# Head of a hybrid-trunk kernel: squares of the input on two engines, meta tokens turned last, a semaphore of its own for the first weight half

## What is computed

```python
meta = jnp.broadcast_to(meta_tokens[None].astype(x.dtype), (bsz, N_META, D_MODEL))
h = jnp.concatenate([meta, x], axis=1)
...
u = rms_norm(h, mix_norm_g[i])          # h * rsqrt(mean(h*h) + eps) * gain, row by row
z = h @ w_in                            # in conv_pool_mixer, on u
a = a_in[..., :CONV_DIM] * jax.nn.sigmoid(a_in[..., CONV_DIM:])
```

## Time and profile before

| | |
|---|---|
| median of 3 runs | 1159.05 us (1157.74 to 1159.46) |
| the profiled execution, its own time | 1157.56 us |
| its span, first to last instruction | 1155.8 us, mean granted TensorE clock 0.994 |
| TensorE matmul busy | 1128.4 us, 98% of the span |
| first matmul of the first projection | 16.19 us after the span's start |

### The profile page before, as it was taken

How to read it: one execution, slowest core, us unless ns; L and a number is a source line. 1 busy time by engine, 2 the same in 40 slices (tenths; PEclk the granted TensorE clock), 3 DMA queues, 4 the chain that set the end, 5 groups by cost and what they waited for, 6 DMA issues and landing times.

```text
span 1155.8 us, 18677 instructions
## 1 busy us (share of the span) xinstructions
PE 1128.4 (98%) x7817; PEld 1050.6 (91%) x7817; DVE 757.6 (66%) x1063; ACT 526.5 (46%) x826; POOL 2.3 (0%) x30
## 2 busy tenths in 40 slices
PE   6999999999999999999999999999989999999997
PEld 6999999999999999999999888787889899899886
DVE  5898887786785785455353345655786786785443
ACT  6435555454454454333443133543454454454332
POOL 0000000000000000000000000000000000000000
PEclk9999999999999999999899999999999999999999
DMA  6322022233224224222113212132224224224311
GB/s 200 111 74 73 1 74 74 74 107 113 74 93 128 74 81 139 91 93 74 57 54 109 74 43 68 37 109 73 73 74 146 73 74 145 74 86 134 109 37 73
DMA packets 98832, 100.29 MB, mean 87 GB/s; under 512 B 2786, under 2 KB 95644, under 8 KB 98748
## 3 DMA queue, kind: packets, MB, share of 16 engines
q1 hardware_dynamic: 98684, 99.02, 27.2%
q10 hardware_dynamic: 64, 0.07, 0.0%
HBM read 96.99 MB, written 2.10 MB: 86 GB/s over the span
## 4 chain that ended last, share of the span: by engine, by line
PE 81%; DVE 8%; ACT 5%; issue 4%; DMA 1%; SPq 0%; DVEq 0%; ACTq 0%
PE ps L1710 48%; PE ps L1897 20%; PE ps L1963 5%; PE ps L1826 3%; DVE relu L1368 2%; ACT w_hi L487 2%; PE ps L2005 1%; PE ps L2020 1%; DVE w_lo L494 1%; ACT w_hi L525 1%; PE ps L1758 1%; ACT c_hi L877 1%; PE ps L1718 1%; ACT parts L890 1%; DMA raw<-in_cp_w_in_dram 1%
## 5 line engine op out<-in xcount | busy, mean ns | idle before, releaser
L1710 PE MATMUL ps<-u_lo,w_hi 128*128 128x272 f32 (+1 forms) x1120 | 299.6, 323 | 2.2 <-DVE u_lo L1206 2.2
L1710 PE MATMUL ps<-u_hi,w_hi 128*128 128x272 f32 (+1 forms) x1120 | 296.0, 320 | 0.0
L1710 PE MATMUL ps<-u_hi,w_lo 128*128 128x272 f32 (+1 forms) x1120 | 295.6, 320 | 0.0
L494 DVE TENSOR_TENSOR w_lo<-raw,w_hi 128x1024 fp32r<-128x1024 f32 x132 | 161.2, 1224 | 122.5 <-ACT w_hi L487 122.5
L487 ACT ACTIVATE w_hi<-raw 128x1024 fp32r<-128x1024 f32 x132 | 138.4, 1052 | 146.3 <-PE ps L1710 135.4
L1710 PEld LDWEIGHTS ps<-u_lo,w_hi 128*128 128x128 f32 x1120 | 184.4, 189 | 20.2 <-issue 5.2
L1710 PEld LDWEIGHTS ps<-u_hi,w_hi 128*128 128x128 f32 x1120 | 185.2, 190 | 16.1 <-issue 1.2
L1710 PEld LDWEIGHTS ps<-u_hi,w_lo 128*128 128x128 f32 x1120 | 184.1, 188 | 15.4
L1897 PE MATMUL ps<-c_lo,w_hi 128*128 128x264 f32 (+1 forms) x672 | 190.4, 283 | 7.3 <-ACT ps L863 4.8
L1897 PE MATMUL ps<-c_hi,w_lo 128*128 128x264 f32 (+1 forms) x672 | 189.9, 283 | 0.0
L1897 PE MATMUL ps<-c_hi,w_hi 128*128 128x264 f32 (+1 forms) x672 | 189.7, 282 | 0.0
(11 more groups left out here) (239 smaller groups left out, 1550.7 us busy)
## 6 DMA issues: line engine op xcount, KB each, us to landing
raw<-in_ffn_w_dram SPq DMA_DIRECT2D x64, 1024.0 KB, 5.4
raw<-in_gla_w_in_dram SPq DMA_DIRECT2D x12, 1024.0 KB, 5.3
raw<-in_cp_w_in_dram SPq DMA_DIRECT2D x8, 512.0 KB, 5.3
raw<-in_cp_w_out_dram SPq DMA_DIRECT2D x4, 1024.0 KB, 5.0
raw<-in_gla_w_out_dram SPq DMA_DIRECT2D x4, 1024.0 KB, 5.3
xin<-in_x_dram SPq DMA_DIRECT2D x4, 512.0 KB, 5.5
raw<-in_cp_w_in_dram SPq DMA_DIRECT2D x2, 1024.0 KB, 5.0
out_dram<-y_tok SPq DMA_DIRECT2D x4, 512.0 KB, 3.0
```

The source lines that it names most:

```text
L494: dve.tensor_tensor(w_view(w_lo, n), half_view(raw, n), w_view(w_hi, n).bitcast(F32), ALU.subtract).then_inc(w_lo_ready, 1)
L1710: last = mm(ps[:, n % NS, c:c + b - a], l, r[:, a - origin:b - origin], start=(k == 0 and i == 0), stop=(k == count - 1 and i == 2))
```

## The change

VectorE squares the meta tokens and tile 1, ScalarE tiles 0, 2 and 3. VectorE writes its unused squares to `squares_dve`. The scaling of the meta tokens goes to GpSimd, as one tensor_scalar. TensorE transposes tiles 0 to 2 for groups k = 0 to 5 only, then the meta tokens, then tile 3 for k = 0 to 5; the eight transposes of groups 6 and 7 (slot ("x", 3)) stand inside the first projection, in front of its third group. The first half of the first weight block has a semaphore of its own, so `split_hi(0)` waits for this half alone; both `split_hi(0)` and `split_lo(0)` also change places with the meta tokens' pieces.

```diff
@@ raw_count
-    return 16 * (b // 2 + 1 + min(b // 2 + 1, B_POOL // 2))
+    return 16 * (b // 2 + 1 + min(b // 2 + 1, B_POOL // 2) - (b % 2 == 0))
@@ split_hi
-            act.wait_ge(raw_loaded[n // 2 % 2], raw_count(n // 2))
+            if n == 0:
+                act.wait_ge(first_loaded, 16)
+            else:
+                act.wait_ge(raw_loaded[n // 2 % 2], raw_count(n // 2))
@@ load_glu
-                      .then_inc(raw_loaded[c % 2], 16)
+                      .then_inc(raw_loaded[c % 2] if n else first_loaded, 16)
@@ GpSimd, at its end
+            pool.wait_ge(meta_rstd, 1)
+            pool.tensor_scalar(meta_normed, xmeta[:, :], rstd_tok[0:META, TT:TT + 1], None, ALU.mult)\
+                .then_inc(meta_normed_ready, 1)
@@ ScalarE (std_of takes the root of tile j's mean, square squares tile j)
+            square(0)
+            std_of(0, x_squared, 1)
+            n = SLOT["gain",]
+            filled(act, n)
+            act.activation(vec[:, 0:2 * KD], ps[:, n % NS, 0:2 * KD], ACT.Copy).then_inc(evac[n % NS], 1)
+            std_of(1, x_squared_dve, 1)
+            square(2)
+            act.wait_ge(meta_summed, 1)
+            act.activation(std_tok[0:META, TT:TT + 1], ms_tok[0:META, TT:TT + 1], ACT.Sqrt,
+                           bias=eps[0:META, :], scale=1.0 / D).then_inc(meta_std, 1)
+            std_of(2, x_squared, 2)
+            square(3)
+            std_of(3, x_squared, 3)
+            split_hi(0)
+            evacuated(act, SLOT["xm",])
+            act.activation(u_hi[:, :, 0:META], u_meta, ACT.Copy).then_inc(u_meta_hi_ready, 1)
@@ VectorE
+            dve.wait_ge(meta_loaded, 16)
+            V.scalar_tensor_tensor(out=squares_dve[0:META, :], in0=xmeta[:, :], scalar=1.0, in1=xmeta[:, :],
+                                   op0=ALU.mult, op1=ALU.mult, accum_out=ms_tok[0:META, TT:TT + 1])\
+             .then_inc(meta_summed, 1)
+            dve.wait_ge(x_loaded[1], 16)
+            dve.wait_ge(meta_summed, 1)
+            V.scalar_tensor_tensor(out=squares_dve, in0=xin[:, 1, :], scalar=1.0, in1=xin[:, 1, :],
+                                   op0=ALU.mult, op1=ALU.mult, accum_out=ms_tok[:, 1:2])\
+             .then_inc(x_squared_dve, 1)
...
+                if j == 1:
+                    dve.wait_ge(meta_std, 1)
+                    V.reciprocal(rstd_tok[0:META, TT:TT + 1], std_tok[0:META, TT:TT + 1]).then_inc(meta_rstd, 1)
@@ TensorE
+            for j in range(TT):
+                if j == TT - 1:
+                    pe.wait_ge(meta_normed_ready, 1)
+                    n = SLOT["xm",]
+                    for k in range(KD):
+                        last = flip(ps[:, n % NS, META * k:META * (k + 1)], meta_normed[:, P * k:P * (k + 1)], META)
+                    last.then_inc(filled_n, 1)
+                pe.wait_ge(x_normed_ready, j + 1)
+                flip_normed(j, 0, KD - 2)
+
+            def flip_last():
+
+                for j in range(TT):
+                    flip_normed(j, KD - 2, KD)
@@ first projection
-                        input_wait if c == 0 else None)
+                        input_wait if c == 0 else None, flip_last if c == 0 else None, 2)
```

More of the change, by code:

```diff
@@ L326, in build_trunk @@
         x_squared = sem("x_squared")
+        x_squared_dve = sem("x_squared_dve")
         x_std = sem("x_std")
@@ L702, in _, with std_of, square @@
             act.activation(std_head[:, 0:1], eps[:, :], ACT.Sqrt)
[L705 to L711, removed]
+            def std_of(j, squared, count):
+                act.wait_ge(squared, count)
+                act.activation(std_tok[:, j:j + 1], ms_tok[:, j:j + 1], ACT.Sqrt, bias=eps[:, :],
+                               scale=1.0 / D).then_inc(x_std, 1)
+            def square(j):
                 act.wait_ge(x_loaded[j], 16)
@@ L1182, in _ @@
             V.memset(pin[:, :, 0:WMAX], 0.0).then_inc(pin_zeroed, 1)
[L1184 to L1195, removed]
-                                    vec[:, V_MIX:V_MIX + KD, None].to_broadcast([P, KD, META]), ALU.mult)\
-                     .then_inc(evac[n % NS], 1)
+            dve.wait_ge(meta_loaded, 16)
@@ new lines, in _ @@
+            for j in range(TT):
+                dve.wait_ge(x_std, j + 1)
+                V.reciprocal(rstd_tok[:, j:j + 1], std_tok[:, j:j + 1]).then_inc(rstd_tok_ready, 1)
+                dve.wait_ge(rstd_tok_ready, j + 1)
+                V.tensor_scalar(x_normed[:, j, :], xin[:, j, :], rstd_tok[:, j:j + 1], None, ALU.mult)\
+                 .then_inc(x_normed_ready, 1)
+                if j == 1:
+                    dve.wait_ge(meta_std, 1)
+                    V.reciprocal(rstd_tok[0:META, TT:TT + 1], std_tok[0:META, TT:TT + 1]).then_inc(meta_rstd, 1)
@@ L1198, in _ @@
+            n = SLOT["xm",]
+            evacuated(dve, SLOT["gain",])
+            filled(dve, n)
+            V.tensor_tensor(u_meta, ps[:, n % NS, 0:KD * META].rearrange("p (k t) -> p k t", t=META),
+                            vec[:, V_MIX:V_MIX + KD, None].to_broadcast([P, KD, META]), ALU.mult)\
+             .then_inc(evac[n % NS], 1)
+            split_lo(0)
             evacuated(dve, SLOT["xm",])
@@ L1201, in _ @@
              .then_inc(u_meta_lo_ready, 1)
-            split_lo(0)
             for k in range(KD):
@@ L1763, in _, with flip_normed @@
             flip(ps[:, n % NS, 0:2 * KD], gain_rows[:, :], 2 * KD).then_inc(filled_n, 1)
-            pe.wait_ge(x_normed_ready, 1)
-            n = SLOT["xm",]
-            for k in range(KD):
-                last = flip(ps[:, n % NS, META * k:META * (k + 1)], meta_normed[:, P * k:P * (k + 1)], META)
-            last.then_inc(filled_n, 1)
-            for j in range(TT):
-                pe.wait_ge(x_normed_ready, j + 2)
-                for k in range(KD):
+            def flip_normed(j, first, last):
+                for k in range(first, last):
                     n = SLOT["x", k // 2]
```

30 lines of the change are left out of this document (13 added, 17 removed).

## The result

The changed kernel takes 1160.89 us (median of 8 runs, 1159.92 to 1163.58) against 1158.39 us before (8 runs, 1156.06 to 1160.95). The ratio is 1.0024 with a 95% interval of 1.0013 to 1.0035: slower by 2.8 us, or 1.5 to 4.1 (the two medians differ by 2.5). The forecast was 1160.3 us and +1.3. The time lies in its range (1159.4 to 1161.4), but partly by luck: the median of the kernel before came out 0.66 us lower in these 8 runs than in the 3 on which the forecast stood (1159.05). The loss is about double the forecast: it lies just beyond the +0.4 to +2.3 that the forecast had with 0.60, and just beyond the 0.2% whose crossing had 0.20. The profiled execution took 1159.92 us, the lowest of the 8; its span is 1158.1 us, 2.3 more than before.

The account below looks back on a forecast made before the run. TensorE, busy 98% of the span, was taken as the bound, so the first projection's start and TensorE's list count. +0.3 (start) +1.0 (transposes) = +1.3 us: 1160.3 us against the median of the runs, range 1159.4 to 1161.4.

Parts of the forecast that it names:

- What bounds it, and that the shift passes through: TensorE, busy 98% of the span, bounds the kernel; a shift of the first projection moves everything behind it.
- Front of the head: Before the projection: VectorE's squares delay the first large transpose to 8.5 us instead of 8.08, losing 0.4 us.
- GpSimd: Meta scaling in the head: 0.9 to 1.6 us from 9.4, ready by 11.1 and hidden until 12.4.
- The prediction's own sign of being wrong: In the changed profile's head: the forecast is wrong if GpSimd's instruction exceeds 1.85 us.
- the start's excess: Start of the first projection: 16.3 to 16.55 us, taken as 0.3 us later than before.
- The first rival: In the head, GpSimd's scaling stops VectorE and delays tile 2, costing 0.05 to 0.8 us; chance 0.17.
- The threshold of 1.85 us: GpSimd's scaling time from which blocking VectorE decides the sign: delay 1.0 us, sum 2.3.
- The second rival: TensorE's clock high from tile 2 on: projection starts at 15.0, time 1158.9 us, or 1157.2; chance 0.15.
- The eight transposes: Groups 6 and 7, inside the first projection: on the path with no cover, where before they were hidden.
- the term of 1.0 us: Cost of the transposes inside the projection: 0.88 us at the high clock and about 0.1 for the change of kind.
- The own semaphore: First weight half: worth nothing; the 0.99 us of waiting removed turns into VectorE's wait for "xm".

Follow-up runs that it names:

- meta_on_vector: Changed kernel with the meta tokens' scaling on VectorE between tiles 2 and 3, none on GpSimd; 1161.12 us against 1157.95 before, ratio 1.0029.
- x3_late_only: Kernel before with only the eight transposes of groups 6 and 7 moved inside the first projection; 1160.12 us against 1157.95, ratio 1.0020.
- x3_ahead: Changed kernel with the eight transposes of groups 6 and 7 in front of the first projection; 1158.27 us against 1157.95 before, ratio 0.9998.
- gpsimd_alone: Kernel before plus the same meta scaling on GpSimd into an unused buffer, at the end of its list; one execution, 1157.97 us.
- own_filled: Kernel before with the first weight half's own semaphore and 13 unread identity transposes ahead of the real ones; 1157.07 us against 1158.04, ratio 0.9989.
- early_meta: Changed kernel, eight transposes ahead of projection, meta root earlier, meta scaling (VectorE) and transposes behind tile 1's; 1158.43 us against 1157.62 before, ratio 1.0006.
- early_meta_filled: early_meta with 22 unread identity transposes ahead of the real ones; 1156.49 us against 1157.62 for the kernel before, ratio 0.9995.
- squares_shared: Kernel before with only the squares of the meta tokens and tile 1 moved to VectorE; 1158.99 us against 1158.04, ratio 1.0005.
- filled_only: Kernel before with only 13 unread identity transposes added ahead of the real ones; 1159.27 us against 1157.62, ratio 1.0011.
- own_semaphore: Kernel before with only the first weight half's own semaphore; 1157.63 us against 1157.95, ratio 0.9998.
- after_again: Changed kernel run once more, nothing edited; 1161.35 us against 1158.04 for the kernel before, ratio 1.0024.
- after_filled: Changed kernel with 22 unread identity transposes ahead of the real ones; 1160.12 us against 1157.62 for the kernel before, ratio 1.0020.

## Why the prediction came out as it did

**What bounds it, and that the shift passes through: right.** 2.24 us at the close of the first projection are 2.3 in the span, and in all 14 profiles the work behind the close keeps its distance from it to 0.1 us from 80 to 225 us. What the prediction did not count on is that the clock takes up to 3.2 us more behind that, by itself, from execution to execution (see "What stays open"). One reading in it was wrong, without consequence: the longest single waits behind the head are not those of the earlier trace rows but two of 2.0 us, for ScalarE (L863) and for VectorE's `c_lo` (L1387).

**Front of the head: right.** Transposes from 8.47 (8.5 forecast), VectorE's square 1.23 and 0.08 for the sum (1.29 forecast), tile 3 scaled at 11.94 (11.7), VectorE standing to 13.65 (13.4), the chain of 3.1 us.

**GpSimd: mis-sized.** "So 1024 elements take 0.9 to 1.6 us" failed: 3.40 us measured, 2.84 alone. The slopes of a memset and an affine select do not carry over to a scaling. It was not hidden: TensorE stood 0.72 us for it in the first profile, and at the low clock it is worth 0.39 us of the start. The prediction's own sign of being wrong, over 1.85 us for GpSimd, had thus come. How much of the start's excess (0.56 late instead of 0.3) is GpSimd's hangs on the clock: `meta_on_vector`, without it, started 0.47 late.

**The first rival, that GpSimd's scaling stops VectorE: half.** Tile 2's scaling took 1.57 us beside GpSimd instead of 0.75, and 0.76 in `meta_on_vector`, where GpSimd stood idle; so the two do disturb each other. But it ended at 11.09 while GpSimd worked to 12.83, and tile 3's took its plain 0.75 in between: neither stood for a whole instruction of the other. The threshold of 1.85 us was passed, yet the chain of this rival did not happen; tile 2 came at 11.09, within 0.1 us of when TensorE asked for it. The Trainium skill, page "SBUF — State Buffer", section "Who interferes with whom", says that whoever issues first holds the shared ports for its whole instruction and that the other is fully blocked. That the two disturb each other agrees with the trace; that it lasts for the whole instruction does not, and the measurement decides.

**The second rival, that TensorE is fast early: its condition came in part.** The clock was high from tile 2 on, but slot "xm" then waited for GpSimd until 12.83, so the start of 15.0 did not come.

**The eight transposes: right in kind, mis-sized.** They are on the path, with no cover, and the larger part of the loss: `x3_late_only` alone is 2.2 us up, `x3_ahead` takes the loss back. "At 1.2 GHz they take 1.7, but then as many matmuls fewer fall into the slow stretch, so its total stays" is the sentence that failed, and with it the term of 1.0 us: they cost 1.70 and 1.2 in the changed kernel's two profiles, and in the first the low clock lasted to 21.7 instead of 19.5. With 0.56 and 1.70 for 0.3 and 1.0, the sum is 2.26 instead of 1.3.

**The own semaphore: right.** In the new order it is worth nothing by the profile, since VectorE stands for slot "xm" until 13.65, two microseconds after the high part is made; no run took it out there. In the old order it gives 0.23 us of the start.

**What stays open: the clock behind the head.** The times fall into steps. The 35 runs of the kernel before, beside these last four, lie at 1156.1 to 1156.3 (12), 1157.5 to 1158.3 (12), 1159.1 to 1159.6 (9) and 1160.9 to 1161.1 (2), some 1.6 us apart, and profiles of one order of work differ in where the granted clock falls, far behind the head too. TensorE by windows, the kernel before and `gpsimd_alone`, whose work there is the same:

```profile
840.00:855.00 15.00, 11.02 (x90) 1.00 0.22 71
```
```profile
840.00:855.00 15.00, 11.78 (x77) 0.77 0.22 71
```

The 14 profiles together show what such a stretch costs. Put VectorE's instructions side by side, each counted from its own run's close of the first projection: from 80 to 225 us every one of the 14 profiles runs with the kernel before to 0.1 us. Differences of more than 0.2 us arise in three places only, and in all of them the granted clock is at half speed in the profile that falls behind. Around 235 us five of them lose 1.5 to 1.6 us (`own_filled`, `early_meta`, `early_meta_filled`, `squares_shared`, `filled_only`), around 850 us eight lose 1.5 to 1.9 us (the last two of these again, `x3_ahead`, `gpsimd_alone`, `own_semaphore`, `x3_late_only`, `after_again`, `meta_on_vector`); a stretch around 550 us costs six of them at most 0.9, and all but 0.2 of that is back at 590. The kernel before, the changed kernel and `after_filled` lose nothing. So from the close to the end of the span there are 1132.1 us without such a stretch, 1133.6 to 1134.1 with one of the two, 1135.3 with both, and one step of the times is about one more of them. The head has two outcomes of its own: in the old order the first projection closed at 23.72 or at 22.23, with and without the low clock in it.

This accounts for the profile of `x3_late_only`: 0.9 us late at the close and 1.8 more behind it, 2.7 in the span. It accounts in the same way for the profile of `filled_only`, 1.5 early and 3.2 late. Whether a kernel's median is moved by such stretches because its head moved, or by chance, the runs do not say: no experiment held the stretches fixed, and why they fall where they do stays open.

## What to carry to other kernels

Work that lies in TensorE's run-up is free only while TensorE stands there anyway; before moving it behind the first matmul, ask what the start really waits for, since here it waited for VectorE's chain and not for these transposes. When a piece goes to another engine, look for an instruction of the same kind on that engine; the slopes of a fill and a select gave a quarter to a half of the price. When one piece comes later, look at what stands behind it in every in-order list: in `squares_shared` ScalarE stood 2.03 us for a piece of 0.31 us, and two tiles behind it came late. And when a change is worth 0.2%, compare the head mark by mark and the rest apart from it: one pair of profiles can agree with a sum to 0.1 us while the rest of the kernel varies by 3.

## What the runs showed of the hardware

- A tensor_scalar of 16 x 1024 float32 takes GpSimd 2.84 us with VectorE idle (`gpsimd_alone`) and 3.40 us beside two scalings of VectorE (both profiles of the changed kernel). VectorE needs 0.74 for the same. Beside GpSimd's, VectorE's own scaling of 128 x 1024 took 1.57 us the first time and 0.75 the second.
- VectorE reads its running sum out in 0.07 to 0.08 us, ScalarE in 0.18 to 0.19.
- The granted clock is written as 1.00 from the first instruction on even where the spacing of equal transposes is 0.213 us and not 0.11; in these traces it says something only behind its first change. In `after_again` it says 1.00 throughout the head while the spacing is the slow one until about 20.5 us.
- The head differs from execution to execution with the same order of work: the first projection closed at 23.72 in the profile before and at 22.23 in `gpsimd_alone`, both starting at 16.19.
- A stretch at half speed around 235 or 850 us costs this kernel 1.5 to 1.9 us, and profiles of the same work differ in whether they have it.
